# Fixed experts for the third pair, its first weights loaded at the write of the routed rows, and later gathers of the last gate rows

## The chip, the core and the metric

The kernel runs on one core of one Trainium2 chip. The metric is the device time of one execution in microseconds (us). All operands are float32.

## The reference

One layer of a diffusion backbone over 384 tokens (128 of context, 256 latent) of width 1024: a mixer (Fourier branch and retention branch), and then a mixture of 64 small experts, which takes more than half of the time and is what the change touches:

```python
def _moe(h, w_router, router_bias, we_g, we_u, we_d, ws_g, ws_u, ws_d):
    t = h.reshape(b * length, d)                       # 384 x 1024
    scores = jax.nn.sigmoid((t @ w_router))            # 384 x 64
    ...                                                # group-limited top 8 of 64 per token
    hid = jax.nn.silu(einsum('td,edf->tef', t, we_g)) * einsum('td,edf->tef', t, we_u)
    routed = einsum('tef,efd->td', hid * combine[..., None], we_d)
    shared = (jax.nn.silu(t @ ws_g) * (t @ ws_u)) @ ws_d
    return routed + shared
x = x + g2 * _moe(h, ...)                              # then the final RMSNorm
```

Each expert has a gate and an up matrix of 1024 x 256 and a down matrix of 256 x 1024, 1 MB (1024 KB) each, so all 64 are 192 such matrices. Every token goes to 8 experts, 3072 assignments in all, 48 per expert on average. `g2` is a row of 1024 gates for context tokens and another for latent ones.

## The kernel before

**Pairs of experts.** The experts are worked on two at a time, 32 pairs, numbered p = 0 to 31. The routed tokens of a pair stand in 128 slots, 64 for each expert; in the last five pairs (27 to 31) the fuller expert has 96 and the other 32, and the five fullest experts are put with the five emptiest. Tokens that find no slot would be handled by further rounds behind pair 31. The order of the experts comes from a sort by number of tokens (VectorE: `key_row`, `key_rank`, `perm`; TensorE turns it into the table `tab_order`, and the semaphore `order_ready` says that it can be read). The experts of `AHEAD`, (4, 5, 6, 7), are out of the sort: they have the first places, so pairs 0 and 1 are known beforehand and their weights are loaded before the routing is done.

**What one pair takes.** POOL gathers the tokens' rows from the DRAM tensor `h2_rows` into `xg` (function `gather`, line 645; each row is 1024 features and 64 routing weights). TensorE turns them (`tokens_of`, lines 1212 and 1215), ScalarE copies them to `xT`. `gate_up(p)` (line 1270) multiplies by the gate and up weights and signals `gate_up_done`; silu and product on ScalarE and VectorE (lines 1645, 2275); `hidden_T` turns the result (line 1281); `down(p)` (line 1295) multiplies by the down weights and signals `down_done`; ScalarE and VectorE split the result into `y_hi` and `y_lo`; `scatter` (line 1313, for the last pairs line 1385) multiplies by the slot matrix `slotT`, which puts the rows back at their tokens, and VectorE adds them up (line 2286).

**TensorE's order** is fixed in the code. For each p from 1 to 30: `gate_up(p)`, `tokens_of(p + 1)`, `slots_of(p + 2)` (while there is one), `hidden_T(p)`, four tiles of `scatter(p - 1)`, `down(p)`, the other two tiles. Then `gate_up(31)`, `hidden_T(31)`, `scatter_two(30)`, `down(31)`, `scatter_two(31)`. ScalarE's order is silu of p, copies of the tokens of p + 1, copy of the hidden rows of p, split of p.

**SyncE (SP) issues the weights** in order (lines 511, 512 and 518). A unit is 2 MB: the gate and up of one expert, or the two down matrices of a pair; three units make a pair. There are seven homes (six in `ring` and the one called `spare`, which is the memory of U), taken in turn; the last two pairs use six only, because `spare` then takes the rows of g2 (`g2_rows`, issued at line 609). `pair_freed` waits until the unit that had the home is used up: for the first unit of pair 2 the home is `spare`, which no pair has had; its second and third unit take the homes of pair 0's gate and up weights and wait for `gate_up_done` 1. Before pair 2 SP waits for `x0_parked` (x's first tile stored to DRAM, issued at line 594) and for `order_ready`.

**POOL** writes h2's rows to `h2_rows` (line 726, three writes, semaphore `h2_written`), then the routing weights beside them (line 728, `w_written`), and after both lands the gathers, in order of the pairs. For the last two pairs the result is multiplied by the g2 gates before the scatter (`remainder_gated`), with one row of gates per slot, gathered by `gather_gates` (line 658) from the DRAM tensor `mod_rows` into memory that held the shared expert's down weights. POOL's loop is `gather(p)` and then, for p = 30 and 31, `gather_gates(p)`.

Of the kernel before, what the change touches and what calls it, by code (L numbers as in the profile page):

```python
# [18 lines left out]
TT = T // P  # L19
# [7 lines left out]
E = 64  # L27
# [5 lines left out]
FSLOTS = 32  # L33
LAST = PAIRS
NEXT = LAST % 2
AHEAD = (4, 5, 6, 7)
UNEVEN = 5
FREE_FIRST = (7, 4, 5, 6, 7, 4)
IN_ORDER = (4, 5, 6, 7, 4, 5)
# [4 lines left out]
SHARED_FROM = 3  # L44
# [28 lines left out]
def constants():  # L73
# [43 lines left out]
    key = -e.astype(float)  # L117
    key[list(AHEAD)] = -1e5 * (1 + a(len(AHEAD)))
    parts["key"] = np.tile(key[None], (P, 1))
    far = a(UNEVEN)  # L120
    sorted_n = E - len(AHEAD)
    order = np.concatenate([a(sorted_n, E), a(UNEVEN, sorted_n - UNEVEN), np.stack([far, sorted_n - 1 - far], 1).ravel()])
# [102 lines left out]
def trunk_kernel(nc, A, outs, consts, dists):  # L225
    y_prompt, y_sample, new_f, new_b = outs
    ctx = ExitStack()
    with ctx:
        home = {}

        def sb(name, shape, dt=F32):
            home[name] = -(-nc.sbuf_base // 32) * 32
            return ctx.enter_context(nc.sbuf_tensor(name, shape, dt))
# [31 lines left out]
        tab_order = sb("tab_order", [1, E], I32)  # L265
# [8 lines left out]
        def sem(name):  # L274
            if name not in sems:
                sems[name] = ctx.enter_context(nc.semaphore(name))
            return sems[name]
# [121 lines left out]
        r_rank = R[:, 6, :, :]  # L399
        ahead_bf = sb("ahead_bf", [E, len(AHEAD)], BF16)  # L400
        further_bf = sb("further_bf", [E, 1], BF16)
# [79 lines left out]
        def computed(eng, name):  # L481

            eng.wait_ge(sem("tile_done"), TILE_AT[name] + 1)
# [6 lines left out]
        def stand_alone(eng, signal):  # L490

            eng.sem_inc(sem(signal), 1)

        def column(table, b):
            return table[:, b:b + 1] if isinstance(b, int) else table[:, bass.ds(b, 1)]
# [10 lines left out]
        def load_gate_up(sp, row, p, n, landed):  # L507

            w = unit(PARTS * p + n)
            src = (lambda a: a[row:row + P, :]) if isinstance(row, int) else (lambda a: a[bass.ds(row, P), :])  # L510
            sp.dma_start(w[:, 0:CELL], src(w_eg)).then_inc(sem(landed), 16)
            sp.dma_start(w[:, CELL:2 * CELL], src(w_eu)).then_inc(sem(landed), 16)

        def load_down(sp, row, p, n, landed):

            w = unit(PARTS * p + 2)[:, n * CELL:(n + 1) * CELL]
            src = w_ed[row:row + P, :] if isinstance(row, int) else w_ed[bass.ds(row, P), :]
            sp.dma_start(w, src).then_inc(sem(landed), 16)

        def pair_freed(eng, u):  # L520

            p, part = divmod(held_by(u), PARTS)
            if part == 2:
                eng.wait_ge(sem("down_done"), 2 * (p + 1))
            else:
                eng.wait_ge(sem("gate_up_done"), p + 1)

        @block.sync
        def _(sp):
# [52 lines left out]
            for n in range(2):  # L582
                load_gate_up(sp, AHEAD[n] * P, 0, n, "gate_up_in0")
            for n in range(2):
                load_down(sp, AHEAD[n] * P, 0, n, "down_in0")
            sp.wait_ge(sem("g2_weighed"), 4)
            load_gate_up(sp, AHEAD[2] * P, 1, 0, "gate_up_in1")
            computed(sp, "mix20")
# [3 lines left out]
                load_down(sp, AHEAD[2 + n] * P, 1, n, "down_in1")  # L592
            sp.wait_ge(sem("x1_ready"), 1)
            sp.dma_start(x0_rows, x[:, 0, :]).then_inc(sem("x0_parked"), 16)
            sp.wait_ge(sem("order_ready"), 1)
            for p in range(2, PAIRS):
                e = [sp.value_load(column(tab_order, 2 * p + n), min_val=0, max_val=E - 1) for n in range(2)]
                for n in range(2):
                    if p == 2 and n == 0:
                        sp.wait_ge(sem("x0_parked"), 16)  # L600
                        computed(sp, "h2T01")
                    else:
                        pair_freed(sp, PARTS * p + n)
                    load_gate_up(sp, e[n] * P, p, n, f"gate_up_in{p % 3}")
                if p == PAIRS - 1:
                    sp.dma_start(x[:, 0, :], x0_rows).then_inc(sem("x0_back"), 16)
                    src = mod_rows[MOD_AT["g2"], :, :].rearrange("c n -> (c n)").rearrange("(o n) -> o n", o=1).broadcast_to([P, 2 * D])
                    sp.wait_ge(sem("g2_stored"), 16)
                    sp.dma_start(g2_rows.rearrange("p c n -> p (c n)"), src).then_inc(sem("g2_rows_in"), 16)
                pair_freed(sp, PARTS * p + 2)  # L610
                for n in range(2):
                    load_down(sp, e[n] * P, p, n, f"down_in{p % 3}")
                if p == 2:
                    computed(sp, "h2T11")
                    sp.dma_start(sd_w[1], w_sd[:, 1, :]).then_inc(sem("shared_in"), 16)
# [33 lines left out]
        def _(pool):  # L649

            def gather_gates(p):

                pool.wait_ge(sem("gate_up_done"), p)
                pool.wait_ge(sem("scattered"), 72)
                pool.wait_ge(sem("slot_kinds"), p - (LAST - 3))
                stand_alone(pool, "passed")
                n = KEEP + 1 + p % 2
                pool.indirect_dma_start(slot_gate[p], None, mod_rows[MOD_AT["g2"], :, :], bass.IndirectOffsetOnAxis(idx[:, n:n + 1], 0),
                                        bounds_check=1, oob_is_err=False).then_inc(sem("gates_in"), 16)
# [76 lines left out]
            for p in range(2, LAST):  # L736
                pool.wait_ge(sem("slots_ready"), p + 1)
                if p == 2:
                    computed(pool, "tokens0b")
                else:  # L740
                    pool.wait_ge(sem("tokens_done"), 2 * (p - 2))
                gather(pool, p % 2, p % KEEP, f"gathered{p % 2}")
                if p in slot_gate:
                    gather_gates(p)
# [977 lines left out]
        def _(dve):  # L1722
# [19 lines left out]
            def weighed(name, j, c):  # L1742
                i, parts, _, _ = SECTION[name]
                w = piece(f"ada{i + j}").rearrange("p (k n) -> p k n", k=KC)
                part = parts[2 * c + j]
                piece_landed(dve, f"ada{i + j}")
                link(v.tensor_scalar(part, w[:, 0, :], condr[:, 0, c:c + 1], None, ALU.mult))
                for k in range(1, KC):
                    ins = v.scalar_tensor_tensor(part, w[:, k, :], condr[:, k, c:c + 1], part, ALU.mult, ALU.add)
                    if k < KC - 1:  # L1750
                        link(ins)
                ins.then_inc(sem(f"{name}_weighed"), 1)

            def row_of(name):
                o = tile(f"{name}s")
                if name == "sc2":
                    dve.wait_ge(sem("states_written"), 32)
                _, _, out, added = SECTION[name]
                if added is None:
                    emptied_by(v.tensor_copy(out, o[:, :]), f"{name}s")  # L1760
                else:
                    dve.wait_ge(sem(f"{name}_bias_in"), 32)
                    emptied_by(v.tensor_tensor(out, o[:, :], added, ALU.add), f"{name}s")
# [721 lines left out]
```

## Time and profile before

| what | value |
|---|---|
| median of 3 runs | 895.19 us (893.06 to 895.57) |
| profiled execution | 895.6 us |
| its span, first to last instruction | 893.8 us |
| TensorE (PE) busy | 868.0 us, 97% |
| VectorE (DVE) busy | 472.6 us, 53% |
| ScalarE (ACT) busy | 166.7 us, 19% |
| GpSimd (POOL) busy | 58.3 us, 7% |
| moved by the 16 DMA engines | 288.00 MB, mean 322 GB/s |

Busy times come from one profiled execution. A busy TensorE is one with a matmul under way, not one at its peak. The page also has the span in 40 slices of 22.3 us, with the GB/s of each slice; from the 18th slice to the 38th they are all between 408 and 422. Below, a row of the timeline is: start in us, duration in us, engine, source line, operation, output <- input, shape, number of instructions merged, and in brackets the idle time before it with what ended it. "SPq" and "POOLq" rows are a queue's own work, such as issuing a DMA. The releasers are inferred from semaphores.

### The profile page before, as it was taken

Reading aid. Unit: us, or ns where it says so; the run is one execution under the profiler, and the core shown is the slowest. Engines: PE = TensorE matmul, PEld = TensorE weight load, DVE = VectorE, ACT = ScalarE, POOL = GpSimd, SP = SyncE. Lnnn points to the kernel's source line nnn. Section 1 sums busy time; section 2 is a strip of 40 time slices with the busy share of each in tenths; the row PEclk is TensorE's granted clock in tenths of the full one; section 3 lists DMA queues with packets and bytes.
Section 4 is the critical chain, followed back from the end, with each engine's and each line's share of the span. In section 5 each row is a group of like instructions: output and inputs, shape, how many; then the busy total and the mean of one; then the engine's idle time right before and its main releaser. Section 6 shows DMA issues by size and latency. Waiting matters only on the chain.

```text
span 893.8 us, 11385 instructions
## 1 busy us (share of the span) xinstructions
PE 868.0 (97%) x4186; PEld 445.6 (50%) x4186; DVE 472.6 (53%) x1031; ACT 166.7 (19%) x349; POOL 58.3 (7%) x75
## 2 busy tenths in 40 slices
PE   7999999999999999999999999999999999999884
PEld 6774446777655547644544444434444444444332
DVE  3645398936796945434443444435444353535447
ACT  4131012020000034121111112112121212111113
POOL 1020100000000000100000000000000000000000
PEclk9999999999999999999999999999999999999998
DMA  9998433512575847499999999999999999999981
GB/s 330 389 368 226 148 125 126 197 50 92 224 279 201 352 192 259 162 408 419 421 418 419 417 419 417 418 418 409 412 421 418 421 418 421 418 420 418 418 328 74
DMA packets 63626, 288.00 MB, mean 322 GB/s; under 512 B 6472, under 2 KB 6528, under 8 KB 38480
## 3 DMA queue, kind: packets, MB, share of 16 engines
q1 hardware_dynamic: 56176, 265.60, 74.8%
q0 software_dynamic: 7392, 21.63, 6.5%
q8 instruction: 35, 0.57, 0.3%
q14 instruction: 23, 0.19, 0.1%
HBM read 287.34 MB, written 4.33 MB: 326 GB/s over the span
## 4 chain that ended last, share of the span: by engine, by line
PE 89%; DMA 8%; DVE 2%; SPq 1%; issue 1%; ACT 0%; DVEq 0%
PE bank L1270 23%; PE bank L834 12%; PE bank L1295 11%; PE bank L827 9%; PE bank L1313 9%; DMA ring<-in_w_exp_up 6%; PE bank L1051 5%; DMA ring<-in_w_ada 2%; PE bank L1212 2%; PE bank L1098 1%; PE bank L1215 1%; PE bank L839 1%; PE bank L844 1%; PE bank L1311 1%; PE bank L1004 1%; PE bank L1006 1%
## 5 line engine op out<-in xcount | busy, mean ns | idle before, releaser
L1270 PE MATMUL bank<-ring,QK 128*64 128x512 f32 (+1 forms) x1056 | 228.3, 602 | 5.8 <-DMA ring<-in_w_exp_up 5.8
L2286 DVE TENSOR_TENSOR hT<-bank,hT 128x512 f32<-128x512 f32 x174 | 109.7, 684 | 83.1 <-PE bank L1313 82.2
L1270 PEld LDWEIGHTS bank<-ring,QK 128*64 128x64 f32 (+1 forms) x1056 | 71.4, 130 | 128.3 <-issue 128.3
L2275 DVE SCALAR_TENSOR_TENSOR VG<-VG,cw,bank 128x256 f32<-128x256 f32 x32 | 15.4, 480 | 170.9 <-issue 164.9
L1295 PE MATMUL bank<-ring,VG 128*64 128x512 f32 (+1 forms) x512 | 102.2, 598 | 0.4 <-ACT VG L1656 0.4
L834 PE MATMUL bank<-hT,ring 128*128 128x384 f32 x256 | 86.0, 489 | 0.0
L827 PE MATMUL bank<-ring,hT 128*128 128x512 f32 x192 | 82.7, 593 | 0.0
L1313 PE MATMUL bank<-y_hi,slotT 128*128 128x512 f32 x180 | 80.9, 449 | 0.0
L1313 PE MATMUL bank<-y_lo,slotT 128*128 128x512 f32 x180 | 70.9, 394 | 0.0
L1663 ACT CAST y_hi<-bank 128x512 fp32r<-128x512 f32 x60 | 32.3, 589 | 195.2 <-PE bank L1313 191.9
L834 PEld LDWEIGHTS bank<-hT,ring 128*128 128x128 f32 x256 | 47.8, 190 | 33.7 <-issue 2.4
L827 PEld LDWEIGHTS bank<-ring,hT 128*128 128x128 f32 x192 | 36.4, 190 | 45.7 <-issue 45.7
L1295 PEld LDWEIGHTS bank<-ring,VG 128*64 128x64 f32 (+1 forms) x512 | 29.4, 130 | 58.3 <-issue 57.8
L1270 PE MATMUL bank<-spare,QK 128*64 128x512 f32 x128 | 56.6, 595 | 0.0
L1313 PEld LDWEIGHTS bank<-y_hi,slotT 128*128 128x128 f32 x180 | 33.8, 188 | 30.7 <-issue 25.7
L1645 ACT ACTIVATE VG<-bank 128x256 f32<-128x256 f32 x32 | 12.3, 385 | 196.3 <-PE bank L1270 196.3
L1051 PE MATMUL bank<-ring,U 128*128 128x512 f32 x96 | 42.0, 593 | 0.0
L2292 DVE TENSOR_TENSOR y_lo<-bank,y_hi 128x512 fp32r<-128x512 f32 x60 | 38.5, 682 | 3.6 <-ACT y_hi L1663 3.5
L1313 PEld LDWEIGHTS bank<-y_lo,slotT 128*128 128x128 f32 x180 | 34.0, 189 | 7.8 <-issue 2.9
L1650 ACT COPY QK<-bank 128x512 f32<-128x512 f32 x62 | 33.3, 589 | 5.6 <-PE bank L1212 5.5
L645 POOL DMA_INDIRECT QK<-h_rows,idx x16 | 15.9, 992 | 218.8 <-DVE idx L2191 190.8
L645 POOL DMA_INDIRECT VG<-h_rows,idx x16 | 16.1, 1005 | 215.3 <-DVE idx L2191 200.2
(425 smaller groups left out, 950.4 us busy)
## 6 DMA issues: line engine op xcount, KB each, us to landing
ring<-in_w_exp_gate SPq DMA_DIRECT2D x56, 1024.0 KB, 12.3
ring<-in_w_exp_up SPq DMA_DIRECT2D x56, 1024.0 KB, 15.1
ring<-in_w_exp_down SPq DMA_DIRECT2D x56, 1024.0 KB, 17.0
ring<-in_w_ada SPq DMA_DIRECT2D x12, 2048.0 KB, 12.2
ring<-in_w_in SPq DMA_DIRECT2D x9, 2048.0 KB, 18.0
spare<-in_w_exp_gate SPq DMA_DIRECT2D x8, 1024.0 KB, 11.2
spare<-in_w_exp_up SPq DMA_DIRECT2D x8, 1024.0 KB, 14.4
spare<-in_w_exp_down SPq DMA_DIRECT2D x8, 1024.0 KB, 18.7
```

The costliest lines, as they stand in the source:

```text
L645: pool.indirect_dma_start(xg[n], None, h2_rows, bass.IndirectOffsetOnAxis(idx[:, k:k + 1], 0), bounds_check=T - 1, oob_is_err=False).then_ ...
L827: ins = mm(o[:, :], h[:, k, t * P:(t + 1) * P], w[:, k, :], start=(k == 0), stop=(k == KC - 1))
L834: ins = mm(o[:, 0:T], w[:, k, m * P:(m + 1) * P], rhs[:, k, :], start=(k == 0), stop=(k == kc - 1))
L1051: ins = mm(o[:, :], mergedT[:, k, t * P:(t + 1) * P], w[:, k, :], start=(k == 0), stop=(k == KC - 1))
L1212: ins = nc.tensor.transpose(lo[:, k * P:(k + 1) * P], xg[n][:, k * P:(k + 1) * P], ident)
L1270: ins = mm(ps[0][rows, :], xT[:, k, rows], gate_up_of(p, n)[:, k, :, :], start=(k == 0), stop=(k == KC - 1))
L1295: ins = mm(ps[2 + h][rows, :], hidT[:, j, rows], down_of(p, n)[:, j, h * 512:(h + 1) * 512], start=(j == 0), stop=(j == 1))
L1313: ins = mm(o, slotT[k][:, t * P:(t + 1) * P], y[:, h * 512:(h + 1) * 512], start=(n == 0 and not shared), stop=(n == 1))
L1650: nc.scalar.copy(halves[n], ps[4 + n][:, :].rearrange("p (k s) -> p k s", k=4)).then_inc(sem("xT_ready"), 1)
L1663: nc.scalar.copy(y_hi[:, h * 512:(h + 1) * 512], ps[2 + h][:, :]).then_inc(sem("hi_ready"), 1)
L2286: v.tensor_tensor(into, o, into, ALU.add).then_inc(sem("summed"), 1)
L2292: v.tensor_tensor(y_lo[:, cut], ps[2 + h][:, :], y_hi[:, cut], ALU.subtract).then_inc(sem("lo_ready"), 1)
```

## The change

`AHEAD` has six experts, so pair 2 is experts 8 and 9 whatever the routing, and the sort covers the other 58. SP's wait for the sort's table moves behind pair 2's loads. For the first unit of pair 2 SP waits for `x0_parked` and for the three writes of h2's rows, in place of the turned tile `h2T01` and the table. POOL's `gather_gates` waits for the end of pair 30's gate and up products for pair 30 (before: the end of pair 29's), and for the arrival of the g2 rows for pair 31 (before: the end of pair 30's products); both also for `scattered` 90 in place of 72.

```diff
-AHEAD = (4, 5, 6, 7)
+AHEAD = (4, 5, 6, 7, 8, 9)
...
             sp.dma_start(x0_rows, x[:, 0, :]).then_inc(sem("x0_parked"), 16)
-            sp.wait_ge(sem("order_ready"), 1)
             for p in range(2, PAIRS):
-                e = [sp.value_load(column(tab_order, 2 * p + n), min_val=0, max_val=E - 1) for n in range(2)]
+                if p == 3:
+                    sp.wait_ge(sem("order_ready"), 1)
+                if 2 * p < len(AHEAD):
+                    e = AHEAD[2 * p:2 * p + 2]
+                else:
+                    e = [sp.value_load(column(tab_order, 2 * p + n), min_val=0, max_val=E - 1) for n in range(2)]
                 for n in range(2):
                     if p == 2 and n == 0:
                         sp.wait_ge(sem("x0_parked"), 16)
-                        computed(sp, "h2T01")
+                        sp.wait_ge(sem("h2_written"), 16 * TT)
                     else:
                         pair_freed(sp, PARTS * p + n)
                     load_gate_up(sp, e[n] * P, p, n, f"gate_up_in{p % 3}")
...
             def gather_gates(p):
 
-                pool.wait_ge(sem("gate_up_done"), p)
-                pool.wait_ge(sem("scattered"), 72)
+                if p == LAST - 2:
+                    pool.wait_ge(sem("gate_up_done"), p + 1)
+                else:
+                    pool.wait_ge(sem("g2_rows_in"), 16)
+                pool.wait_ge(sem("scattered"), 6 * (SHARED_FROM + 12))
                 pool.wait_ge(sem("slot_kinds"), p - (LAST - 3))
```

`gate_up_done` is raised by one at the end of each pair's gate and up products, so it is p + 1 when those of pair p are done. `LAST` is 32, `TT` is 3, `SHARED_FROM` is 3.

## Rows read from the trace of the kernel before

**Rows 1.** Busy time by stage: length, each engine, granted clock, DMA share, GB/s.
```profile
380.00:796.00 416.00, 415.16 (x1949) 179.92 (x1948) 182.62 (x394) 78.54 (x164) 25.76 (x26) 1.00 1.01 417
863.40:866.80 3.40, 3.40 (x20) 1.10 (x24) 0.81 (x2) 0.08 (x1) 0.30 (x1) 0.61 0.78 296
```

**Rows 2.** Chain of waits, pairs 26 and 27: start, duration, line of the products.
```profile
781.34 7.02 PE bank L1270 x32
796.59 7.05 PE bank L1270 x64
```

**Rows 3.** Waits, whole span: us in total, times, longest.
```profile
PE bank L1270 <- DMA ring<-in_w_exp_up: 5.8, 4, 2.6
```

**Rows 4.** Timeline around the sort and pair 0.
```profile
356.79 0.53 POOL L726 DMA_DIRECT2D h_rows<-VG  x1 [5.08 <-ACT VG L1587]
...
360.40 0.77 POOL L728 DMA_DIRECT2D h_rows<-S  x1 [3.07 <-DVE S L2171]
...
364.70 1.21 POOL L645 DMA_INDIRECT VG<-h_rows,idx  x1 [3.54 <-DVE idx L2191]
...
370.58 0.66 PE L1212 MATMUL bank<-consts_sb,VG 128*128 128x128 f32 x4
...
372.58 0.37 SPq L511 DMA_DIRECT2D spare<-in_w_exp_gate  x1
...
379.96 0.33 SPq L511 DMA_DIRECT2D ring<-in_w_exp_gate  x1
```

**Rows 5.** DMA issues, windows 356.5:360, 360:363, 363:366: size, us to landing.
```profile
h_rows<-VG POOLq DMA_DIRECT2D x1, 512.0 KB, 2.9
...
h_rows<-S POOLq DMA_DIRECT2D x1, 96.0 KB, 2.2
...
VG<-h_rows,idx POOLq DMA_INDIRECT x1, 4.5
```

**Rows 6.** Busy time by stretch around the first load of pair 2.
```profile
372.00:376.00 4.00, 3.60 (x18) 1.31 (x20) 1.34 (x4) 0.35 (x1) 1.01 (x2) 1.00 0.77 250
376.00:380.00 4.00, 4.00 (x21) 1.31 (x18) 0.00 (x0) 0.18 (x1) 0.14 (x1) 1.00 0.98 398
380.00:384.00 4.00, 3.16 (x24) 2.10 (x24) 1.19 (x5) 2.10 (x6) 0.00 (x0) 1.00 0.92 341
```

**Rows 7.** POOL's DMA queue in 366 to 372 us: packets, MB, share.
```profile
q0 software_dynamic: 144, 0.46, 25.7%
```

**Rows 8.** Timeline of the last two pairs.
```profile
836.29 0.99 POOL L658 DMA_INDIRECT AB<-mod_rows,idx  x1 [11.94 <-PE bank L1270]
...
839.09 0.99 POOL L645 DMA_INDIRECT QK<-h_rows,idx  x1 [1.81 <-DVE idx L2195]
...
845.57 7.07 PE L1270 MATMUL bank<-ring,QK 128*32 128x512 f32 x64 [1.96 <-DMA ring<-in_w_exp_up]
...
852.57 0.66 PE L1212 MATMUL bank<-consts_sb,QK 128*128 128x128 f32 x4
...
853.54 0.99 POOL L658 DMA_INDIRECT Fm<-mod_rows,idx  x1 [13.46 <-PE bank L1270]
...
860.38 0.40 PE L1313 MATMUL bank<-y_lo,slotT 128*128 128x512 f32 x1
...
863.38 8.77 PE L1270 MATMUL bank<-ring,QK 128*32 128x512 f32 x64 [2.60 <-DMA ring<-in_w_exp_up]
...
867.03 1.22 DVE L2351 TENSOR_TENSOR hT<-hT,U 128x1024 f32<-128x1024 f32 x1 [2.82 <-DMA U<-mod_rows]
```

**Rows 9.** DMA issues (whole span, then 836:846, us to landing) and POOL's queue, 836:846.
```profile
VG<-h_rows,idx POOLq DMA_INDIRECT x16, 8.8
...
q0 software_dynamic: 219, 0.73, 18.3%
...
AB<-mod_rows,idx POOLq DMA_INDIRECT x1, 9.7
QK<-h_rows,idx POOLq DMA_INDIRECT x1, 10.1
```

## The prediction

> **What bounds the kernel now.** Read the busy times by stage first: from 380 to 796 us the DMA engines are full at 417 GB/s, and TensorE is busy 415.16 of the 416 us [rows 1]. Two resources are full at once, so the next view is which of them is ahead. A pair of experts needs 6 x 1024 KB = 6.29 MB of weights and a gather of its rows, 0.46 MB by the one gather that has its stretch to itself [rows 7]; 6.75 MB at 417 GB/s is 16.2 us. TensorE's period in the chain of waits is 796.59 - 781.34 = 15.25 us [rows 2]. The transfers are slower by 1 us a pair, start with a lead (two pairs loaded ahead), and lose it slowly: the waits put the whole of TensorE's loss to weights at 5.8 us in 4 waits [rows 3], and the two long ones lie at the very end, 1.96 us before pair 30's gate and up products and 2.60 us before pair 31's [rows 8]; the other two are 1.2 us together. Behind the last one there is a second price: the granted clock of 863.4 to 866.8 is 0.61 of full, the level of 1.2 GHz for most of it, so that pair 31's gate and up products take 8.77 us where pair 30's took 7.07 [rows 1, 8]. What is to be won here is thus the 5.8 us and the 1.7 us of clock, 7.5 us; what can be lost is whatever stops TensorE, since it has no slack elsewhere.
>
> The profiled execution took 895.6 us with a span of 893.8, so 1.8 us lie around the span. The median of three runs is 895.19, 0.4 below. A difference of 0.3% (2.7 us) is about what a measurement of this kernel can tell from none.
>
> **Part 1: two more fixed experts.** Experts 8 and 9 take the fourth and fifth place in the order. Counting the reference's routing on its inputs gives them 34 and 59 tokens; both fit in the 64 slots of a place, neither is among the five fullest (65 to 73) or the five emptiest (27 to 30) that make the uneven pairs, and the list of those pairs stays as it is. So no further rounds arise and each place does the same instructions as before. Two more copies of a 64x1 column on VectorE, long before the routing: 0.
>
> **Part 2: what the earlier load brings.** Pair 2 has three units of weights, but only the first (gate and up of its first expert, 2.1 MB, home "spare") has a free home. The second and third wait in `pair_freed` for `gate_up_done` 1, as now, and they are issued at 379.96 [rows 4], right when pair 0's products end. Nothing behind them in SP's order moves either. So the question is how much of the first unit is still on the engines at 380. It was issued at 372.58; in 372 to 380 the engines moved 250 x 4 + 398 x 4 = 2.59 MB [rows 6], of a total of 2.10 MB of weights and two gathers of 0.46 MB [rows 7], 3.02 MB: 0.43 MB are left, 1.0 us at 417 GB/s. After 380 the engines now lose (417 - 341) x 4 / 417 = 0.7 us [rows 6] while the second unit starts up behind that rest. With the change the rest is gone, but the start-up, an estimate of 1.5 us (the 96 KB write lands 2.2 us after its issue, 0.2 us of it transfer and the rest on both sides of it) [rows 5], lies bare. Net: 1.0 + 0.7 - 1.5 = 0.2 us earlier for every later load. The bounds are 0 and 1.0 us; I take 0.2. The other 5 us of this load were hidden before and are hidden after, under TensorE's 7 us of pair 0.
>
> **Part 3: what the earlier load puts in the way.** SP now waits for the three writes of h2's rows in place of the sort. The last is issued at 356.79 and lands 2.9 us later, 359.7 [rows 4, 5], so the load is issued at about 360.0 (an estimate of SP's reaction) and occupies the engines until about 366.5 to 367 (2.1 MB, 5.0 us, and its start-up). Queued beside it is the write of the routing weights, issued at 360.40, which takes 2.2 us on idle engines; POOL waits for it ahead of the first gather, issued at 364.70 and landing in 4.5 us at 369.2; TensorE takes it up at 370.58 [rows 4, 5]. Cover: POOL is held until 363.7 by the slot numbers (the gather starts 1.0 us after), so the write has 363.7 - 362.6 = 1.1 us, and the gather 370.58 - 369.2 = 1.4 us: together 2.5 us. The write is 96 KB [rows 5]; sharing the engines evenly with the load it needs as much again, 0.2 us, and with a few of the load's rows ahead of each of its own perhaps 1 us. That is covered; I take 0. If it waited for the whole load it would land at 367, the gather would be issued at 368.0 and land at 372.5, and TensorE would be 1.9 us late, with all that follows. Bounds 0 and 1.9.
>
> **Part 4: the gate gathers.** This is where the size is. POOL's order is gather of pair 30, gates of pair 30, gather of pair 31, gates of pair 31. Now the gates of pair 30 wait for `gate_up_done` 30, the end of pair 29's products; they are issued at 836.29 and pair 31's row gather at 839.09, landing 9.7 and 10.1 us later, at 846.0 and 849.2, ahead of 852.57 where TensorE turns pair 31's tokens [rows 8, 9]. With the change the gates wait for `gate_up_done` 31, the end of pair 30's products. Queued behind that wait on POOL is the row gather of pair 31, and `tokens_of(31)` is TensorE's very next work after pair 30's products. Everything of pair 30 behind it (turning the hidden rows, four tiles of scatter, the down products) comes later in the same order.
> - Gain ahead of it: the low-priority bytes leave the stretch before 845.5. The POOL queue moved 0.73 MB in 836 to 846 us [rows 9], 1.75 us at 418 GB/s; with the 0.2 of part 2 pair 30's weights are there 1.95 us earlier, just when TensorE is free (the wait was 1.96 [rows 8]). Its products run 843.6 to 850.7 in place of 845.57 to 852.64. -1.9 us.
> - Stall: POOL issues the gates 0.9 us after the products' end (853.54 - 852.64, as the gates of pair 31 show) at 851.6, and the row gather 0.99 us of issue plus 0.75 us of preparing later, at 853.35. The engines are still full there (pair 31's weights). Landing takes 8.8 us for a gather alone beside the stream, 10.1 for one close behind the gates [rows 9], and perhaps 12 as it now stands 1.7 us behind them and not 2.8; 4.5 us on idle engines is the far bound below [rows 5]. I take 10.1, the row with the same two transfers: 863.45. TensorE idles from 850.7 to 863.5.
> - Behind it: from 852.57 to the earliest start of pair 31's products are 860.78 + 0.36 - 852.57 = 8.6 us [rows 8]; so 872.0. By then the weights are long there (863.3 at the latest).
> - Clock: a gap of 2.60 us was followed by 0.61 over 3.4 us, a gap of 1.96 us by full clock (7.07 us) [rows 1, 8]. After nearly 13 us of idling I take the same 1.7 us as the price, now in the scatter and down products, with bounds of 0 and 3.4. So 873.7, and 7.07 us at full clock end at 880.8. Before, this end was 863.38 + 8.77 = 872.15. The difference is +8.65 us.
> - The gates of pair 31 wait for `g2_rows_in`, which VectorE sees at 867.0 [rows 8]; issued then they leave the stretch before 863, worth 1.25 us of stream that nobody waits for any more, and land by 877, while they multiply pair 31's down products, which now come behind 880.8. The new condition on `scattered` (90 in place of 72) is met after the scatter of pair 14, some 15 pairs earlier. Gates of pair 30: landed at about 861.3, wanted at about 871: 0.
> From the end of pair 31's products on, nothing changes: 21.65 us to the end of the span.
>
> Sum: 895.6 + 8.65 + 0 (part 3) + 0 (part 1) = 904.2, against the median 895.19 + 8.65 = 903.8. I say 904.0.
>
> **The rivals.**
> Rival A, the other side: the gates cease to compete and nothing waits for the row gather, since it gets out ahead of the wait. Then pair 31's weights land 1.75 + 1.25 us earlier, TensorE runs through to 861.1, keeps its clock and ends pair 31's products at 868.2, 4 us earlier: 891.2; with the whole 2.1 MB of the early load won as well (if the stream at 380 really stood behind them) all 7.5 us: 888. It decides at one point: whether the gather of pair 31 has landed by the end of pair 30's products. Against it: POOL's order in the code and in the rows, 836.29 ahead of 839.09, and the 0.2 us of part 2. Chance 0.05.
> Rival B: the stall comes but the gather lands as on idle engines, 4.5 us. Then 857.9, products at 866.5 + 1.7, end at 875.2: +3.1, 898.3. Against it: all transfers of 380 to 866 stand beside a full stream; the median of a row gather is 8.8 [rows 9]. Chance 0.05.
> Rival C: as forecast, and the write of the routing weights is held by the whole load (part 3): +1.9 on top, 906. For it: no row excludes it, and the cover of 2.5 us is thin. Chance 0.18.
> Rival D, the change does nothing to be measured: stall and clock are bought back by both gains. It would need a landing within 4 us and no clock loss. Chance 0.02.
> The forecast itself: 0.70.
>
> **How the numbers follow.** The forecast's own spread: landing 8.8 to 12 us (-1.3, +1.9), clock 0 to 3.4 (-1.7, +1.7), stream gain 0 to 1.0 (-0.0 of the end, since TensorE is then the later one): 901 to 907.5. With rival C and its spread up to 909. B, A and D hold 0.12 and are left out below. Range 900.5 to 908.5. Slower by over 0.3%: 0.70 + 0.18 + 0.05 = 0.93; within: 0.02; faster: 0.05.
>
> **What would show it.** In the profile after: POOL's gates of pair 30 start after pair 30's products and the row gather under 2 us behind; a wait of TensorE's line 1212 for that gather of about 12 us; the waits for weights before pairs 30 and 31 gone; granted clock near half just behind the new wait, and a full-clock 7.07 us for pair 31. At the front: the spare load issued at about 360, the next at about 380.0, and the first turning of tokens still at 370.6 (rival C: 372.5). The forecast falls if the row gather is seen landed before pair 30's products end, or if its landing time with two gathers in a row is far from 10 us.

## The result and the profile after

| | before | after |
|---|---|---|
| median of 6 runs | 894.89 us (893.06 to 895.57) | 908.83 us (907.87 to 910.8) |
| profiled execution | 895.6 us | 909.53 us |
| its span | 893.8 us | 907.7 us |

The ratio is 1.0161, with a 95% interval of 1.0147 to 1.0175 (it is taken from the single runs, so it can differ a little from the ratio of the medians): the change makes the kernel 13.9 us slower. The direction was forecast, the size was not: 904.0 was predicted and 908.5 was the upper end of the range.

The waits of TensorE come first. In the kernel after (us in total, times, longest):

```profile
PE bank L1219 <- DMA QK<-h_rows,idx: 13.2, 1, 13.2
...
PE bank L1219 <- DMA VG<-h_rows,idx: 2.2, 1, 2.2
```

and from its page the group of the gate and up products (busy, mean ns, idle before):

```profile
L1277 PE MATMUL bank<-ring,QK 128*64 128x512 f32 (+1 forms) x1056 | 228.1, 598 | 0.6 <-DMA ring<-in_w_exp_up 0.6
```

The waits for weights have gone from 5.8 us [rows 3] to 0.6. In their place stand two waits for gathered rows, 13.2 and 2.2 us; the first is pair 31's, the second pair 0's. All line numbers behind line 600 are 4 or 7 higher than before: line 1219 is the old 1212, 1277 the old 1270.

The timeline of the last two pairs, after (compare [rows 8]):

```profile
847.81 7.07 PE L1277 MATMUL bank<-ring,QK 128*32 128x512 f32 x64 [0.63 <-DMA ring<-in_w_exp_up]
...
855.79 0.99 POOL L665 DMA_INDIRECT AB<-mod_rows,idx  x1 [27.34 <-PE bank L1277]
857.09 0.99 POOL L649 DMA_INDIRECT QK<-h_rows,idx  x1 [0.30 <-issue]
868.05 1.12 PE L1219 MATMUL bank<-consts_sb,QK 128*128 128x128 f32 x4 [13.16 <-DMA QK<-h_rows,idx]
...
870.46 0.99 POOL L665 DMA_INDIRECT Fm<-mod_rows,idx  x1 [12.38 <-DMA U<-mod_rows]
...
878.60 7.07 PE L1277 MATMUL bank<-ring,QK 128*32 128x512 f32 x64
```

Pair 30's products end at 854.88. Then POOL issues the gates and, 1.30 us behind them, the row gather of pair 31, and TensorE stands until 868.05. Before, these two were issued at 836.29 and 839.09, and TensorE turned pair 31's tokens without a wait. What follows the wait runs slowly at first (1.12 us for four matmuls that take 0.66); busy times and granted clock behind it, after:

```profile
868.05:871.45 3.40, 3.40 (x13) 3.19 (x14) 0.06 (x1) 1.45 (x3) 0.99 (x1) 0.50 0.45 188
871.45:874.85 3.40, 3.40 (x18) 1.70 (x20) 2.71 (x4) 0.00 (x0) 0.00 (x0) 0.62 0.53 208
```

The granted clock (third column from the end) is 0.50, that is 1.2 GHz, for 3.4 us and more, and full again before pair 31's products, which take 7.07 us.

The timeline of the front, after (compare [rows 4]):

```profile
360.87 0.33 SPq L511 DMA_DIRECT2D spare<-in_w_exp_gate  x1
...
361.50 0.77 POOL L735 DMA_DIRECT2D h_rows<-S  x1 [3.07 <-DVE S L2178]
...
369.33 1.07 POOL L649 DMA_INDIRECT VG<-h_rows,idx  x1 [7.06 <-DMA h_rows<-S]
...
371.33 0.27 PE L1195 MATMUL bank<-perm,consts_sb 64*1 64x64 f32 x2
...
373.91 0.63 PE L1219 MATMUL bank<-consts_sb,VG 128*128 128x128 f32 x4 [2.15 <-DMA VG<-h_rows,idx]
...
376.15 8.55 PE L1277 MATMUL bank<-ring,QK 128*64 128x512 f32 x32
384.63 0.66 PE L1219 MATMUL bank<-consts_sb,QK 128*128 128x128 f32 x4
...
384.75 0.33 SPq L511 DMA_DIRECT2D ring<-in_w_exp_gate  x1
```

and the DMA issues in 360 to 363 us, after (size, us from issue to landing; compare [rows 5]):

```profile
spare<-in_w_exp_gate SPq DMA_DIRECT2D x1, 1024.0 KB, 4.9
spare<-in_w_exp_up SPq DMA_DIRECT2D x1, 1024.0 KB, 7.5
h_rows<-S POOLq DMA_DIRECT2D x1, 96.0 KB, 7.0
```

Read the last line with the timeline: the write of the routing weights, 2.2 us before, takes 7.0 and lands at 368.5, within 0.2 us of the load's end (361.24 + 7.5 = 368.7). POOL waited 7.06 us for it, the first row gather goes out at 369.33, and TensorE waits 2.15 us for that. Pair 0's products then take 8.55 us and not 7.09, at a granted clock of 0.61 in their first 4 us:

```profile
376.00:380.00 4.00, 4.00 (x14) 1.28 (x14) 1.34 (x4) 0.00 (x0) 0.98 (x1) 0.61 0.01 4
```

The same marks in the timeline of before, which [rows 4] and [rows 8] don't have:

```profile
370.22 0.27 PE L1188 MATMUL bank<-perm,consts_sb 64*1 64x64 f32 x2
...
379.70 0.66 PE L1212 MATMUL bank<-consts_sb,QK 128*128 128x128 f32 x4
...
835.32 0.66 PE L1212 MATMUL bank<-consts_sb,VG 128*128 128x128 f32 x4
```

With them the whole difference of the two spans is laid out (us):

| stretch | before | after | difference |
|---|---|---|---|
| start to the sort's last products | 370.22 | 371.33 | +1.11 |
| from there to the turning of pair 0's tokens | 0.36 | 2.58 | +2.22 |
| from there to the end of pair 0's products | 9.12 | 10.72 | +1.60 |
| from there to the end of pair 29's products | 455.62 | 454.27 | -1.35 |
| from there to the start of pair 30's products | 10.25 | 8.91 | -1.34 |
| from there to the turning of pair 31's tokens | 7.00 | 20.24 | +13.24 |
| from there to the start of pair 31's products | 10.81 | 10.55 | -0.26 |
| pair 31's products | 8.77 | 7.07 | -1.70 |
| from there to the end of the span | 21.65 | 22.03 | +0.38 |
| sum | 893.8 | 907.7 | +13.9 |

The first line can't be put down to the change: in the profiled executions of the five kernels below whose front is that of before, the same mark lies between 369.9 and 371.8 us.

### The profile page after: what moved, and what is told of

Read it like the earlier page. It is cut to its first block, busy times and chain, and to the rows that moved or that the text cites. A ratio compares the mean times of both kernels' runs of the same rounds, so it can differ in the third digit from the quotient of the medians.

```text
span 907.7 us, 11373 instructions
## 1 busy us (share of the span) xinstructions
PE 871.7 (96%) x4186; PEld 447.4 (49%) x4186; DVE 473.1 (52%) x1033; ACT 166.8 (18%) x349; POOL 58.1 (6%) x75
## 4 chain that ended last, share of the span: by engine, by line
PE 91%; DMA 5%; DVE 2%; issue 1%; ACT 1%; SPq 0%; POOL 0%; POOLq 0%; ACTq 0%; DVEq 0%
PE bank L1277 24%; PE bank L1302 12%; PE bank L841 12%; PE bank L1320 9%; PE bank L834 9%; PE bank L1058 5%; DMA ring<-in_w_exp_up 2%; PE bank L1219 2%; PE bank L1222 1%; DMA QK<-h_rows,idx 1%; PE bank L846 1%; PE bank L1288 1%; PE bank L851 1%; PE bank L1318 1%; PE bank L1105 1%; PE bank L1011 1%
## 5 line engine op out<-in xcount | busy, mean ns | idle before, releaser
L2194 DVE TENSOR_SCALAR slotT<-bank,consts_sb 128x384 fp32r<-128x384 f32 x32 | 19.8, 618 | 19.7 <-PE bank L1160 17.7
```

The costliest lines, as they stand in the source:

```text
L2194: v.tensor_scalar(slotT_k, o_rank, cols[:, slot_col:slot_col + 1], None, ALU.is_equal).then_inc(sem("slot_found"), 1)
```

## The experiments

**The two parts, each alone.** The first kernel has the six fixed experts and the early load, with `gather_gates` as before; the second has only the new `gather_gates`.

```diff
 # e1_front, against the kernel after
-                if p == LAST - 2:
-                    pool.wait_ge(sem("gate_up_done"), p + 1)
-                else:
-                    pool.wait_ge(sem("g2_rows_in"), 16)
-                pool.wait_ge(sem("scattered"), 6 * (SHARED_FROM + 12))
+                pool.wait_ge(sem("gate_up_done"), p)
+                pool.wait_ge(sem("scattered"), 72)
```

> The front of the change alone: pair 2 fixed, its first unit loaded when h2's rows are written; the gate gathers as before. Theory F (the early load holds up the write of the routing weights, and with it the first row gather and TensorE): the write lands about 7 us after its issue and not 2.2, the first row gather is issued at about 369, TensorE waits about 2.2 us at line 1219's first use and pair 0's products take 8.55 us in place of 7.09 at a lower granted clock; +3.8 us there, of which the first two waits for weights (1.3 us) give back: +2.5 us, 0.3%. Rival (the front is covered as the prediction had it, everything lies in the last pairs): 0 to -0.2 us.

> The later gate gathers alone, with four fixed experts and the load of pair 2 after the sort as before. Theory G (the row gather of pair 31 is queued behind the gates' wait on POOL): TensorE waits 13 us for it after pair 30's products; +10 us, 1.1%. Rival (the gates cost little by themselves and the front's delay makes the end bad): +5 us or less. If F and G are both right and independent, the two parts alone sum to about the +13.9 us of the change.

Measured, against 894.22 us of before: the front alone 897.78, ratio 1.0042 (1.0023 to 1.0060), +3.6 us where +2.5 was expected; the gates alone 904.47, ratio 1.0117 (1.0094 to 1.0140), +10.3 us where +10 was expected. The intervals are 2.1 to 5.4 us and 8.4 to 12.5 us. Their sum is 13.8, and the change costs 13.9, so within about 3 us the two parts add up and no third is needed. In the profile of the front alone the write takes 6.9 us, the wait is 2.82 us and pair 0's products 9.99 us, longer than in the change (this was the slowest of its seven runs):

```profile
PE bank L1216 <- DMA VG<-h_rows,idx: 2.8, 1, 2.8
...
377.16 9.99 PE L1274 MATMUL bank<-ring,QK 128*64 128x512 f32 x32
```

In that of the gates alone the wait is 13.1 us. Both theories hold; both rivals (0 to -0.2 us for the front, +5 us or less for the gates) are out.

**The front: what exactly is held up.** Three kernels with the front alone, which move the early load or halve it.

```diff
 # e5_behind_w
-                        sp.wait_ge(sem("h2_written"), 16 * TT)
+                        sp.wait_ge(sem("w_written"), 16)
 # e7_behind_gather
-                        sp.wait_ge(sem("h2_written"), 16 * TT)
+                        sp.wait_ge(sem("gathered0"), 16)
 # e6_half: for the first unit of pair 2, in place of load_gate_up
+                        sp.dma_start(first[:, 0:CELL], w_eg[...]).then_inc(sem("gate_up_in2"), 16)
+                        sp.wait_ge(sem("order_ready"), 1)
+                        sp.dma_start(first[:, CELL:2 * CELL], w_eu[...]).then_inc(sem("gate_up_in2"), 16)
```

> The front alone, with the early load issued when the routing weights are written and not when h2's rows are. Theory F (what the load held up was the 96 KB write): the write lands 2.2 us after its issue again and the first row gather is issued at about 365 to 366. The gather now stands beside the load: if it ends with the load it lands at about 372, TensorE waits 0.5 to 1 us, and the whole is +0.5 to +1 us; if it gets an even share it lands at about 370.5 and the whole is 0. Rival (not the write but something else of the front costs the 3.6 us): still +3 us or more.

> The front alone with half the early load: the gate matrix (1 MB) when h2's rows are written, the up matrix behind the sort. Theory F, in the form that the small write ends only when the load ahead of it has ended: the load ends 2.5 us earlier, the write lands about 4.5 us after its issue and not 7.0, the first row gather is issued at about 367 and lands at about 371.4, just where TensorE is; 0 to +0.5 us. Rival (the write is only slowed, by some fixed amount, wherever the load ends): 7 us and +3.6 us as before.

> The front alone with the early load issued when the first row gather has landed, still about 2 us ahead of where the sort lets it go. Theory F: write 2.2 us, gather 4.5 us, no wait of TensorE; the load was hidden before and is hidden now: 0 to -0.5 us. If the early load were worth its 5 us of transfer: -3 us or more.

Measured, against 894.37: behind the write 895.16, ratio 1.0009 (0.9994 to 1.0023); half the load 893.91, ratio 1.0001 (0.9989 to 1.0012); behind the gather 894.64, ratio 1.0008 (0.9993 to 1.0023). None differs from before, and all are free of the 3.6 us. The DMA issues of the three, first with half the load, then behind the write, then behind the gather:

```profile
spare<-in_w_exp_gate SPq DMA_DIRECT2D x1, 1024.0 KB, 5.0
h_rows<-S POOLq DMA_DIRECT2D x1, 96.0 KB, 4.7
```

```profile
h_rows<-S POOLq DMA_DIRECT2D x1, 96.0 KB, 2.3
...
VG<-h_rows,idx POOLq DMA_INDIRECT x1, 7.1
```

```profile
h_rows<-S POOLq DMA_DIRECT2D x1, 96.0 KB, 2.2
...
VG<-h_rows,idx POOLq DMA_INDIRECT x1, 4.6
```

So the write of 96 KB takes 2.2 to 2.3 us with nothing beside it, 4.7 with 1 MB ahead of it and 7.0 with 2 MB: behind a load it lands within 0.3 us of that load. It is held to the load's end and not slowed by a share or a fixed amount. POOL's DMA queue shows it too. Its packets in 363 to 366 us and in 366 to 369 us, in the kernel after:

```profile
q0 software_dynamic: 4, 0.02, 1.3%
...
q0 software_dynamic: 44, 0.08, 7.1%
```

These 48 are the write's own packets; none of them moves before 365.7, 4.2 us after the issue, when 178 of the load's 288 have moved. Alone, all 48 move within 2.1 us of the issue.

Behind the write the load meets the gather instead: 7.1 us in place of 4.5, and TensorE waits 1.29 us (pair 0's products then take 8.60 us, so the clock is lost again); that is +0.8 us by the medians, which the interval does not separate from none. And the load behind the gather, still 3 us ahead of where the sort would let it go, wins nothing that can be measured, and nor does the halved one. An earlier first load has no worth here that these runs can tell.

**The gates: the wait or the bytes.** Three kernels with the front of before. In the first both gathers of gates are issued behind both row gathers (`gates_in` is then two semaphores, one for each pair); in the second only the gates of pair 31 wait longer; in the third the row gather of pair 31 waits like the gates of pair 30, but goes ahead of them.

```diff
 # e3_rows_first: the new gather_gates, and
                 gather(pool, p % 2, p % KEEP, f"gathered{p % 2}")
-                if p in slot_gate:
-                    gather_gates(p)
+            for p in slot_gate:
+                gather_gates(p)
 # e4_gates31: the new gather_gates, but
-                    pool.wait_ge(sem("gate_up_done"), p + 1)
+                    pool.wait_ge(sem("gate_up_done"), p)
 # e9_wait_only: e3_rows_first, and ahead of the row gather
+                if p == LAST - 1:
+                    pool.wait_ge(sem("gate_up_done"), LAST - 1)
```

> The later gate gathers with the same conditions, but the row gather of pair 31 is issued ahead of both on POOL; the front as before. Theory G: the wait of 13 us is gone, the gates' bytes leave the stretch ahead of pair 30's and pair 31's weights (1.25 us each), the waits for weights shrink from 5.8 to about 3.3 us and with the last gap under 2 us the clock is kept, 1.7 us: -4.2 us, -0.5%. Rival (it is the late gates themselves that hold up pair 30 and 31, not the row gather behind them): +5 us or more.

> Only the gates of pair 31 later (on the arrival of the g2 rows); those of pair 30 and the front as before. The gap before pair 31's products shrinks from 2.60 to about 1.35 us. Theory K (the lower clock behind that gap depends on its length): the products take 7.07 us and not 8.77; -2.9 us, -0.3%. Rival (the clock falls there whatever the gap): -1.25 us, -0.1%.

> The later gate gathers, front as before; POOL makes the row gather of pair 31 wait for the end of pair 30's products too, but issues it ahead of the gates. Theory G (what costs is where the row gather stands, and of it the wait is the larger part, the gates ahead of it the smaller): it is issued 0.9 us behind the products, 1.3 us earlier than with the gates ahead, and lands in about 8.8 and not 10.8 us; TensorE waits 9.7 and not 13.1 us: +6.9 us. Rival (the gates' bytes ahead of it are the cause): +2 us or less.

Measured: rows first 893.63 against 894.22, ratio 0.9993 (0.9980 to 1.0005); only pair 31's gates 893.13 against 894.22, ratio 0.9985 (0.9972 to 0.9998); the wait without the gates ahead 901.55 against 894.37, ratio 1.0088 (1.0063 to 1.0113), +7.2 us where +6.9 was expected. The order on POOL is the cause, shown from both sides: with the same late gates and the row gather ahead of their wait the 10.3 us are gone, and with the row gather behind the wait but ahead of the gates most of them are back. TensorE's waits and the issues of the last kernel, then the issues of the gates alone:

```profile
PE bank L1217 <- DMA QK<-h_rows,idx: 9.6, 1, 9.6
...
QK<-h_rows,idx POOLq DMA_INDIRECT x1, 8.6
AB<-mod_rows,idx POOLq DMA_INDIRECT x1, 11.0
```

```profile
AB<-mod_rows,idx POOLq DMA_INDIRECT x1, 8.5
QK<-h_rows,idx POOLq DMA_INDIRECT x1, 10.8
```

Whichever of the two gathers is issued first lands after 8.5 to 8.6 us, the one 1.3 us behind it after 10.8 to 11.0. Having the gates ahead costs pair 31's rows 2.2 us of landing and 1.3 us of issue, the 3.5 us between the waits of 13.1 and 9.6.

My -4.2 us for the rows first was wrong; -0.6 was measured. The gates of pair 30, moved from 836 to 852 us, leave the stretch ahead of pair 30's weights but enter the one ahead of pair 31's, so only the bytes of pair 31's gates left the stream. The wait before pair 30 fell to 0.30 us, the one before pair 31 stayed:

```profile
844.32 7.07 PE L1273 MATMUL bank<-ring,QK 128*32 128x512 f32 x64 [0.30 <-DMA ring<-in_w_exp_up]
...
861.73 8.68 PE L1273 MATMUL bank<-ring,QK 128*32 128x512 f32 x64 [2.22 <-DMA ring<-in_w_exp_up]
```

The -2.9 us expected of pair 31's gates alone were wrong too; -1.1 was measured, the size that the rival gave. In the profile theory K looks right all the same: the gap before pair 31's products is 1.39 us and they take 7.07 and not 8.77:

```profile
861.58 7.07 PE L1273 MATMUL bank<-ring,QK 128*32 128x512 f32 x64 [1.39 <-DMA ring<-in_w_exp_up]
```

But the profiled execution of before, which gave the 8.77, is itself 1.4 us above the median that the -1.1 is measured against. So the runs show what the bytes are worth and not the 1.7 us of clock.

**Both parts in a harmless form.** The front with the load behind the first row gather, and only pair 31's gates later; beside it the latter alone a second time.

> Both parts in their harmless form: six fixed experts with the early load behind the first row gather, and only the gates of pair 31 later. Theory: the front is worth nothing (0 to -0.3 us), the gates of pair 31 leave the last stretch (1.25 us), and where the clock is kept behind the last gap 1.7 us more: -1 to -3 us, about as the gates alone. Rival (the early load adds a lead of its own once nothing stalls): 2 us or more better than the gates of pair 31 alone.

> Only the gates of pair 31 later, a second time beside the kernel with both parts: -1.1 us again, with an interval that leaves 1 out. Rival (the first time was the scatter of the runs): within 0.1% of before.

Measured, against 894.57: both 893.11, ratio 0.9979 (0.9968 to 0.9990); the gates of pair 31 alone 893.03, ratio 0.9992 (0.9978 to 1.0005). The medians differ from that of before by 1.5 us each, and from each other by nothing: the front adds no lead. The second run of the gates alone has an interval that holds 1, so of a gain of about 0.1% only the combination and the first run say that it is there. I would keep pair 31's gates later and drop the rest.

## Why the prediction was half right

**What bounds the kernel; the rival with the gain.** Right. Once something else delayed TensorE, the waits for weights fell from 5.8 to 0.6 us, and the kernel was no faster for it. Rival A (the row gather gets out ahead) is refuted by the profile and by the pair of kernels above.

**Part 1, the fixed experts.** Right as far as shown: with the load out of the way (`e7_behind_gather`) six fixed experts cost nothing that can be measured.

**Part 2, what the load brings.** Right in kind: the early load was hidden before. The forecast of 0.2 us lies below what these runs can tell.

**Part 3, what the load puts in the way: the step that failed.** I took 0 and kept 1.9 us as the bound, with a chance of 0.18 (rival C). It was rival C, and its price was larger than its bound: +3.6 us with the front alone. As a path rival C was right to 0.3 us: it had the first turning at 372.5, and it is at 373.91, or 372.8 without the 1.1 us by which the whole execution was late there. Three things were off. The choice: I let the small write share the engines with the load, "perhaps 1 us"; it is held to the load's end. The Trainium skill's rule ("DMA: Bandwidth & Descriptors", section "Queues, rings and completion order": turns between queues go by whole packets of many descriptors) agrees in kind with the landings of 2.2, 4.7 and 7.0 us, since a small write does wait out a run of a load's pieces; that it waits out the whole of two 1 MB loads is what the traces show, and the rule alone doesn't say. It was the better guide than my even share, for which no row stood. The end of the load: I had the write landing at 367, that is 6.6 us after its issue, and it was 7.0. And the clock: I priced the stall at the end with a lower clock behind it and forgot the same behind the stall at the front. Pair 0's products took 8.55 us for 7.09, 1.5 us on top of a wait of 2.2 (9.99 in `e1_front`, 2.9 on top of 2.8). In the table the two stretches make 2.2 + 1.6 = 3.8 us, of which 1.35 come back up to pair 29, where the small waits for weights vanish: 2.5 us net in that one execution, and 3.6 by the medians of the front alone.

**Part 4, the gates.** Right in mechanism, and the sum came out, but in part by luck: its terms missed both ways. By its terms, forecast and measured with the gates alone or after:

| term | forecast | measured |
|---|---|---|
| POOL's issue behind the products' end | 0.9 us | 0.91 (after) |
| row gather behind the gates | 1.74 us | 1.30 (after) |
| landing of the row gather | 10.1 us | 10.9 (after), 10.8 (gates alone) |
| TensorE's wait | 12.8 us | 13.2 (after), 13.1 (gates alone) |
| from the turning to pair 31's products | 8.6 us, and 1.7 for the clock: 10.3 | 10.55 (after), 9.70 (gates alone) |
| pair 30's products earlier | 1.9 us | 1.3 (after), 1.7 (gates alone) |
| pair 31's products | 7.07 us | 7.07 |

The landing and the issue missed in opposite ways and nearly cancel. The 8.6 us are 0.4 too long: they add a gap of 0.36 behind a scatter product that is already counted whole, and in `e4_gates31` the stretch without its wait is 861.58 - 1.39 - 852.00 = 8.2. The clock thus cost 2.4 us in the change and 1.5 with the gates alone, for 1.7. The sum was forecast as +8.65 us. In the profile of the gates alone the stretch from the start of pair 29's products to the end of pair 31's is 874.11 + 7.07 - 828.69 = 52.49 us; before it was 872.15 - 828.31 = 43.84: +8.65, the forecast to the last digit, which is chance. In the profile of the change the same terms, from the end of pair 29's products on, make -1.34 + 13.24 - 0.26 - 1.70 = +9.9. The medians say +10.3. Of the 1.6 us between 8.65 and 10.3, 1.1 is that the profiled execution of before, on which the sum was made, lay 1.4 above the median it is compared with (895.6 against 894.2), and that of the gates alone 0.3 above its own; why, stays open.

```profile
828.69 7.07 PE L1273 MATMUL bank<-ring,QK 128*32 128x512 f32 x64
...
874.11 7.07 PE L1273 MATMUL bank<-ring,QK 128*32 128x512 f32 x64
```

These are the two marks in the timeline of the gates alone; that of before for pair 29:

```profile
828.31 7.07 PE L1270 MATMUL bank<-ring,QK 128*32 128x512 f32 x64 [0.44 <-DMA ring<-in_w_exp_up]
```

**The range.** The forecast's own spread ended at 907.5, and with rival C's 1.9 us on top that is 909.4; the working says "up to 909", and the range stopped at 908.5. So the measured 908.8 lies outside the range that was named, and inside the sum behind it. With the measured 3.6 us for the front in place of 0 the forecast is 907.6. By the two profiles the span came out 5.3 us above the forecast (907.7 against 893.8 + 8.65): 1.1 up to the sort, 3.8 at pair 0, -1.35 up to pair 29, 1.3 in the last pairs (9.9 for 8.65) and 0.4 behind them. The step that failed is the largest term; without the other 1.3 and 1.1 the time would still have been inside.

## What to carry to other kernels

An in-order queue that waits for a late event holds everything queued behind it: when an issue is moved later, look first for the next issue on that queue that someone waits for, and put it ahead. A bulk load that is started early because its memory and its data are free is not free for the small transfers issued just behind it: if a chain of short dependent steps (write, gather, products) passes through there, start the load behind the chain. And price a stall of TensorE with the slow clock behind it, wherever it stands: behind the two stalls of this change it cost 1.5 and 2.4 us. As a term of the range, though, since it did not follow every short gap.

## What the runs showed of the hardware

- A write of 96 KB on POOL's queue, issued 0.2 to 0.6 us behind a load on SP's, lands with the load: 2.2 us alone, 4.7 behind 1 MB, 6.9 to 7.0 behind 2 MB. A gather of 0.46 MB issued 2.0 us behind the first half of a 2 MB load took 7.1 us and not 4.5.
- Beside a full stream the first of two gathers lands in 8.5 to 8.7 us and the second, 1.3 us behind it, in 10.8 to 11.0. With 2.8 us between them, as before, they take 9.7 to 10.0 and 10.1 to 10.4 us (before and the seven kernels that issue them so).
- Whether TensorE's clock falls behind a gap did not follow from the gap's length, nor from its place. Before pair 31's products the granted clock of the next 3.4 us fell to 0.61 behind a gap of 2.60 us (before), to 0.67 behind 2.58 (`e7_behind_gather`) and to 0.52 behind 2.22 (`e3_rows_first`); it stayed full behind 1.39, 1.20 and, in the front alone, 2.73 us. Before pair 30's it fell to 0.58 behind 2.38 (`e5_behind_w`) and to 0.51 behind 2.48 (`e6_half`), and stayed full behind 2.14 (`e8_both`) and 2.92. What decides it is open. Three lines: pair 31's in the front alone, pair 30's with the gates of pair 31 alone, second run, and pair 30's in `e5_behind_w`:

```profile
869.26 7.07 PE L1274 MATMUL bank<-ring,QK 128*32 128x512 f32 x64 [2.73 <-DMA ring<-in_w_exp_up]
```

```profile
846.76 7.07 PE L1273 MATMUL bank<-ring,QK 128*32 128x512 f32 x64 [2.92 <-DMA ring<-in_w_exp_up]
```

```profile
848.72 8.77 PE L1274 MATMUL bank<-ring,QK 128*32 128x512 f32 x64 [2.38 <-DMA ring<-in_w_exp_up]
```

- The executions of one kernel differ in the same way. The 69 fast ones of before that ran beside the experiments have mean granted clocks of 0.990 to 0.998 and spans of 890.3 to 894.9 us, and in all three batches the longer spans go with the lower clocks (correlation -0.4 to -0.8). So a loss of clock read from one profile, like the 1.7 us of pair 31, is not the kernel's in each execution.
